# Later gate table, later turns and evenly spread row gathers in the expert pass of a two-block transformer kernel

## The reference, cut to what matters

```python
def peer_ffn(u, w_q, sub_keys, u_tab, v_tab):
    ...
    q = (xt @ w_q).reshape(T, H, 2, PEER_DKEY // 2)
    s = jnp.einsum('thcd,hcnd->thcn', q, sub_keys)
    top_s, top_i = lax.top_k(s, K)
    cand = (top_s[:, :, 0, :, None] + top_s[:, :, 1, None, :]).reshape(T, H, K * K)
    cand_i = (top_i[:, :, 0, :, None] * PEER_NKEYS + top_i[:, :, 1, None, :]).reshape(T, H, K * K)
    best_s, best_j = lax.top_k(cand, K)
    expert = jnp.take_along_axis(cand_i, best_j, axis=-1)
    g = jax.nn.softmax(best_s, axis=-1)
    ...
        act = jax.nn.gelu(jnp.einsum('cd,chkd->chk', xc, u_tab[ec]), approximate=False)
        return jnp.einsum('chk,chkd->cd', gc * act, v_tab[ec])
```

## Time and profile before

| | us |
|---|---|
| median of 3 runs | 2643.46 |
| the three runs | 2641.51, 2643.46, 2649.43 |
| the profiled execution, its own time | 2642.07 |
| its span | 2640.3 |
| PE busy in the span | 2516.8 (95%) |
| POOL busy | 1352.0 (51%) |
| DVE busy | 1625.1 (62%) |
| ACT busy | 1007.5 (38%) |
| first expert pass on PE | 1372.8 to 2039.5 |

### The profile page before, as it was taken

One profiled execution on the slowest core, in us unless ns is written; L12 is line 12 of the kernel. 1 busy time (PEld: TensorE's weight loads), 2 busy tenths in 40 slices (PEclk: granted clock), 3 DMA queues, 4 the chain that ended last, 5 costly groups with the idle time before them and its releaser, 6 DMA issues.

```text
span 2640.3 us, 34192 instructions
## 1 busy us (share of the span) xinstructions
PE 2516.8 (95%) x13121; PEld 2092.5 (79%) x13121; DVE 1625.1 (62%) x2821; ACT 1007.5 (38%) x1768; POOL 1352.0 (51%) x675
## 2 busy tenths in 40 slices
PE   6989999999999899998999799999998999999998
PEld 5656788888788566787789799999998777777776
DVE  4965664153223777563899956777644666666665
ACT  3225422223212555343544255555533333333333
POOL 4410255454432111443435566666677877777774
PEclk9979999999999999999999899999999999999999
DMA  3200122322421000232225579999998988889884
GB/s 130 96 32 1 64 92 83 112 95 80 162 96 65 17 33 33 90 118 96 80 78 158 167 235 305 326 315 321 312 363 327 377 315 314 302 319 325 306 312 183
DMA packets 151781, 477.61 MB, mean 181 GB/s; under 512 B 14688, under 2 KB 47840, under 8 KB 140640
## 3 DMA queue, kind: packets, MB, share of 16 engines
q1 hardware_dynamic: 114784, 341.64, 36.7%
q0 software_dynamic: 36864, 134.23, 14.0%
HBM read 423.39 MB, written 52.43 MB: 180 GB/s over the span
## 4 chain that ended last, share of the span: by engine, by line
PE 73%; DVE 17%; DMA 4%; ACT 2%; POOL 2%; issue 1%; SPq 0%; ACTq 0%; DVEq 0%
PE bank_pair L2122 19%; PE bank_pair L260 13%; PE bank_pair L261 13%; PE bank_pair L262 13%; PE bank_pair L2092 3%; DVE cacc L460 3%; PE bank_pair L2133 2%; PE bank_pair L640 1%; PE bank_pair L1223 1%; DMA u_raw<-expert_u 1%; PE bank_pair L625 1%; POOL w_lo L252 1%; DVE att_e L1460 1%; DMA ug<-expert_u_rows,idx_u 1%; DVE one_hot L2239 1%
## 5 line engine op out<-in xcount | busy, mean ns | idle before, releaser
L252 POOL TENSOR_TENSOR w_lo<-w_raw,w_hi 128x2048 fp32r<-128x2048 f32 (+2 forms) x96 | 426.6, 4444 | 720.4 <-ACT w_hi L247 720.1
L1819 POOL TENSOR_TENSOR u_lo<-u_raw,u_hi 128x1024 fp32r<-128x1024 f32 x128 | 312.0, 2438 | 219.8 <-ACT u_hi L1815 218.9
L1861 POOL TENSOR_TENSOR v_lo<-v_raw,v_hi 128x1024 fp32r<-128x1024 f32 x128 | 310.1, 2427 | 108.9 <-ACT v_hi L1857 108.4
L260 PE MATMUL bank_pair<-uh,u_lo 128*128 128x384 f32 x1024 | 353.0, 345 | 12.6 <-POOL u_lo L1819 12.2
L2342 DVE TENSOR_TENSOR h_lo<-h_raw,h_hi 128x384 fp32r<-128x384 f32 x128 | 236.4, 1847 | 177.8 <-ACT h_hi L1866 173.6
L261 PE MATMUL bank_pair<-ul,u_hi 128*128 128x384 f32 x1024 | 344.0, 336 | 0.0
L262 PE MATMUL bank_pair<-uh,u_hi 128*128 128x384 f32 x1024 | 344.0, 336 | 0.0
L260 PE MATMUL bank_pair<-xh,w_lo 128*128 128x512 f32 x688 | 274.6, 399 | 24.9 <-DVE xl L401 13.6
L247 ACT ACTIVATE w_hi<-w_raw 128x2048 fp32r<-128x2048 f32 (+2 forms) x96 | 174.7, 1820 | 310.0 <-PE bank_pair L262 284.6
L1857 ACT ACTIVATE v_hi<-v_raw 128x1024 fp32r<-128x1024 f32 x128 | 135.6, 1059 | 379.2 <-PE bank_pair L2122 345.6
L261 PE MATMUL bank_pair<-xl,w_hi 128*128 128x512 f32 x688 | 271.2, 394 | 0.0
(11 more groups left out here) (399 smaller groups left out, 5138.8 us busy)
## 6 DMA issues: line engine op xcount, KB each, us to landing
w_raw<-w_small SPq DMA_DIRECT2D x80, 1024.0 KB, 4.8
u_raw<-expert_u SPq DMA_DIRECT2D x128, 512.0 KB
v_raw<-expert_v SPq DMA_DIRECT2D x128, 512.0 KB
h_scratch<-h_act SPq DMA_DIRECT2D x128, 192.0 KB
g_scratch<-stage SPq DMA_DIRECT2D x24, 1024.0 KB, 6.0
g_in<-g_scratch SPq DMA_DIRECT2D x16, 1536.0 KB, 13.6
h_raw<-h_scratch SPq DMA_DIRECT2D x128, 192.0 KB
w_raw<-w_small SPq DMA_DIRECT2D x8, 768.0 KB, 4.2
```

The lines of the kernel that those rows point to most:

```text
L252: pool.tensor_tensor(wl[g % 2][:, :n], raw[g % 2][:, :n], wh[g % 2][:, :n].bitcast(F32), ALU.subtract).then_inc(sem("lo_done"), 1)
L260: pe.matmul(out, al, bh, start=(k == 0), stop=False)
L1819: pool.tensor_tensor(u_lo[c % 2][:, :, :], u_raw[c % 4][:, :, :], u_hi[c % 2][:, :, :].bitcast(F32), ALU.subtract)\
L1861: pool.tensor_tensor(v_lo[c % 4][:, :], v_raw[c % 4][:, :], v_hi[c % 4][:, :].bitcast(F32), ALU.subtract)\
```

## The change

It moves the beginning of the gate table from chunk 32 to chunk 36, so PRE grows by four and POST shrinks from 24 to 20 chunks. The three later transposes of the key lists move from behind chunks 21, 24 and 27 to behind chunks 25, 29 and 33. Gathers 4 to 127 are issued four to every three chunks from chunk 32 on; before it was six to every five from chunk 28 and, behind the table, eight to every five. On DVE the first two batches of hits and rows now stand ahead of the first four dots.

```diff
-        PRE = 32
+        PRE = 36
         EXP_AT = 14
-        TURN_AT = (21, 24, 27)
+        TURN_AT = (25, 29, 33)
...
         def gathers_by(c):
 
-            if c < 28:
+            if c < 33:
                 return max(0, min(UG_EARLY, c - 18))
-            if c < PRE + MID:
-                return UG_EARLY + (c - 27) * 6 // 5
-            return min(P, 96 + (c - PRE - MID) * 8 // 5)
+            return min(P, UG_EARLY + (c - 31) * 4 // 3)
...
             link(dve.tensor_copy(iota_ps, iota_key[:, :]))
             numbers = iota_ps.unsqueeze(1).to_broadcast([P, BT, NK])
-            for j in range(UG_EARLY):
-                dot(j)
             dve.wait_ge(sem("pk_idx"), QT)
             dve.tensor_copy(idx_v[:, :], lin_bank[0][:, 3 * P:4 * P]).then_inc(sem("pk_idx"), 1)
             for n in range(2):
                 mark_hits(n)
                 mark_rows(n)
+            for j in range(UG_EARLY):
+                dot(j)
```

## The result

| | before | after |
|---|---|---|
| median | 2644.09 us (4 runs) | 2626.44 us (4 runs) |
| lowest to highest | 2641.51 to 2649.43 | 2625.78 to 2629.34 |
| the profiled execution | 2642.07 | 2626.50 |
| its span | 2640.3 | 2624.8 |

The ratio is 0.9933, with a 95% interval of 0.9919 to 0.9947: 17.7 us faster, and by the interval between 14 and 21. Forecast were 2628 and a gain of 15.6 us.

What follows compares the result with a forecast made beforehand. The prediction took the head as bound by DVE's keys and the tail by transfers. Gains of 9.4 us (head) and 6.2 us (tail), with the middle at 0, sum to 15.6 us, giving 2628 us, range 2618 to 2641.

Steps and rivals of the forecast that it cites:

- The keys: Head, DVE: a stretch of keys takes 12.6 us plus 2.07 for each POOL low part beside it.
- The turns: Head: PE's 9.6 us wait for tile 1's keys goes; turn 1 waits 0.4 us and turn 2 1.4.
- Gather 4 and the low part of chunk 34: Head, POOL: gather 4 waits for tile 3's keys, delaying the low part behind it; PE waits 4.3 us.
- Gather 7: Head, POOL: gather 7 waits for dot 0, delaying chunk 35's low part; PE waits 0.7 us.
- Gather 11: One chunk behind chunk 37: gather 11 needs dot 4, behind batch 0 on DVE; PE waits 1.4 us at chunk 38.
- the slow clock: Head: TensorE's slow pace behind the two longest waits, two before and one after; some 1.8 us more gain.
- the head term: Head: waits fall from 19.9 to 12.3 us, 7.6 less, plus 1.8 of slow pace; 9.4 us gained.
- The middle at nothing: Middle, beside the gate table: PE busy throughout, 359 GB/s asked in phases with stores; cost put at 0.
- slower rival: Middle, store phases between chunks 48 and 108: bound by transfers at 313 GB/s, 31.5 us more, 2660 us; chance 0.07.
- The tail's book: Tail: bytes asked against 409 GB/s, excess 6.25 MB before, 3.71 after, 1.3 absorbed by buffers; 6.2 us gained.
- The rival without stretched keys: Head: DVE's keys not stretched by low parts, turns never wait; 3.6 us more gain, 2624 us; chance 0.10.
- Only the head counts: Tail: the fetch for the second pass, with last gathers in its way, gives back the tail's gain; 2634 us; chance 0.16.

Runs made afterwards that it cites:

- tiny low parts: Changed kernel with POOL's subtraction for chunks 22 to 33 cut to 16 of 1024 elements in a partition; 2630.7 us (1 run), kernel before 2645.7.
- uneven gathers: Changed kernel with gathers six for five chunks up to chunk 107, then two for each chunk; 2637.9 us, kernel before 2643.0.
- even gathers alone: Kernel before with only its gathers changed, 32 for 25 chunks from chunk 28; 2640.2 us against 2643.0, again 2640.8 (1 run) against 2645.7.
- the last run: Changed kernel, ACT scaling first hits behind turn 2, gathers from 4 one chunk later (11 for 8), three for two from chunk 40; 2611.8 us, ratio 0.9876.

## Why the prediction was right, and where not

The sign and the mechanism came out, and the time lies at 2626.4 us inside 2618 to 2641. The forecast's 9.4 us from the head include the wait at chunk 38, which lies in the middle; measured are 9.4 - 1.8 = 7.6 us. The tail gained 6.0 us where 6.2 were forecast, with a spread of 1 to 2. So the pass gained 2.0 us less than the 15.6 of the sum, and the medians 2.1 us more. That the time is so near to 2628 is in part luck.

**The keys.** Forecast were 23.0 us with five low parts and 18.8 with three; measured 23.2 and 18.3. The run with tiny low parts shows the cause: 12.8 us with POOL almost out of the way. The Trainium skill, page "SBUF — State Buffer", section "SBUF: two separate sides", describes the ports that VectorE and GpSimd share as an exclusive lock for a whole instruction. The trace agrees in kind: both the keys and the low parts beside them take longer (7.47 us for two low parts that take 2.4 us each alone). Keys 1 were mis-sized: two more low parts beside them, not one, 29.0 us instead of 27, which cost nothing, since PE came later still.

**The turns.** The first waits nothing, the others 0.9 and 1.1 us; forecast were 0.4 and 1.4. With the turns alone put back, 13.1 us of head were lost again, more than the head had gained, and the time was that of the kernel before.

**Gather 4 and the low part of chunk 34.** Forecast 4.3 us, measured 4.2, with POOL's 5.76 us idle ahead of it.

**Gather 7.** Forecast was a wait of 0.7 us at chunk 35 and that the order on DVE costs up to a microsecond. Putting the order back changed the head by 0.3 us the other way: nothing that the trace can tell.

**Gather 11.** Forecast 1.4 us, measured 1.67.

**What the walk left out, and the slow clock.** A low part beside the keys is itself held up by DVE, and PE waited 1.26 us for that of chunk 29. Still, all waits of PE together fell from 21.0 to 14.0 us, 7.0 less where 7.6 were forecast. So most of the 1.8 us by which the head term fell short lies, by difference, in the slow clock, from which the sum had 1.8 us back: 7.6 - 7.0 leaves 0.6. Behind the wait of 4.2 us the granted clock was 0.76 from 1520 to 1528 and 0.81 from 1528 to 1536, for which the sum had only 1.2 us.

**The middle at nothing.** Right at 4/3. The slower rival's step, that 313 GB/s might be all that a mix with stores can do, is refuted: 392 GB/s, with a store among them, passed without a wait of PE. Its other door, dots that are late for the ring of seven buffers, is real, but at the beginning of the table and not in the phases of stores.

**The tail's book.** The difference of 6.2 us was right, the fitted number was not. The tail of the kernel before begins with the last table half at 1924, not at 1928, so 115.5 - 24 x 4.16 = 15.7 us were lost there and not 12.1. The 6.25 MB of the book at 409 GB/s are 15.3 us: the buffers absorb nothing that shows. For the changed kernel the book then says 3.71 / 0.409 = 9.1 us, and 92.9 - 20 x 4.16 = 9.7 were measured. For the uneven gathers it said 22.7 and 103.3 - 83.2 = 20.1 were measured. For the even gathers alone it failed, by 5 and 7 us in two executions. It holds bytes and knows nothing of TensorE's clock; and since the clock fell in the tails of the changed kernel (0.79 in one window of 8 us, behind a wait of 3.1 us) and of the uneven gathers (0.79 in two) as well, its good fit there is in part luck.

**The rival without stretched keys** was priced at 3.6 us more. The run with tiny low parts shows 1.1 in the head: the rival's walk overlooked that the chain over dot 0 ends almost as late.

**Only the head counts** did not come: the gates landed in 13.6 us, and the tail gained its 6.0 us.

What stays open is the 4 us between the 13.6 that the pass gained in the two traces and the 17.7 between the medians: 2.9 at the start less 1.0 in the rest, and 2.1 by which the profiled executions lie nearer to each other than the medians. The start of the pass, with the same instructions ahead of it, moves by 5 us between executions; the runs show that it moves and not why.

## What to carry to other kernels

When a wait is moved to a later place in a program, walk each queue past it: here the wait for the keys vanished on PE and came back on POOL, in front of PE's own operands, at less than half the price. A stall can also help another engine: here POOL stood still while PE did, and DVE's keys ran faster for it. Ask whether such a relief goes away with the stall. Where transfers bind, add up the bytes asked for per step against the rate that the trace shows, then spread what can be moved. And where an edit has no effect, try it again once the engine that would profit from it asks earlier.

## What the runs showed of the hardware

TensorE's clock can make fewer waits nearly as dear as many. In the kernel before, twelve waits of at most 1.7 us, 11.1 in all, left it at full speed (2.4 GHz). With the even gathers alone, seven waits of 6.9 us in all, the longest 3.0, came with up to 5.1 us of lost clock, in the same two places in two executions. The length of a wait does not decide it alone: one of 2.81 us left the clock at 1.00 (uneven gathers), and behind one of 1.85 us it fell (the last run). The page "TensorE: Matmul & The Clock Gate" of the Trainium skill, section "What's actually happening", has the clock set by how busy the engine has been of late. The traces agree with that in so far as each of these falls stands at a wait.

A low part of 2.4 us on POOL cost the keys on DVE, mostly bf16 work, some 2 us: they took 12.8 us beside tiny ones, 18.3 beside three and 23.2 beside five. DVE's work stretched the low part in turn, to 7.47 us for two. The 16 DMA engines carried up to 418 GB/s in the windows shown, and 392 in one of 20 us in which PE never waited. A DMA share of 1.00 is no sign of that ceiling: the kernel before shows it at 350 GB/s from 1826 to 1842.
